# The gate and the squares of a grouped norm moved into the scan before it, its roots into the transposes

## The chip, the cores and the metric

The program runs on one core of a Trainium2 chip, as one launch. The metric is the device time of the execution in microseconds (us), the median of several runs. The engines are PE (TensorE, matmuls), DVE (VectorE), ACT (ScalarE), POOL (GpSimd) and SP (SyncE, which issues most transfers here). They run on their own and wait for each other by semaphores.

## What is computed

One layer of a diffusion backbone on 640 tokens (128 context and 512 latent tokens, five chunks of 128), all in float32. What matters here is the Mamba-2 branch, cut to the part around the change:

```python
y_f, h_f = _ssd_chunked(xh, dt[0], a_neg[0], bm, cm, h0_f)
y_r, h_b = _ssd_chunked(_flip_seq(xh), ...)
y = y_f + _flip_seq(y_r) + xh * d_skip
y = _group_rmsnorm(y * jax.nn.silu(z), norm_w, SSD_GROUPS)   # 4 groups of 512 of the 2048 channels
...
merged = sigmoid(gate_a) * (y_a @ w_branch_a) + sigmoid(gate_b) * (y_b @ w_branch_b)
```

`_group_rmsnorm` divides each group of 512 channels of a token by the root of its mean square (plus 1e-6) and multiplies by the weight of the channel. silu(z) was computed earlier and lies in DRAM (`silu_z`). After this branch come the output projection, a second norm, the router and the mixture of experts.

## The kernel before

The kernel is written by hand, stage by stage. A stage is one block in which each engine has its own list of instructions in program order; between two stages all engines meet. An engine works strictly down its list, so a wait holds up all that stands behind it. The three stages that matter follow each other:

- `stage_ssd`, the scan. It runs over 40 sub-steps, in the order of the list `subs`: chunk (0, then 4, 3, 2, 1), group of 512 channels, half of a group. Two sub-steps, a pair here, make one group of one chunk. In a sub-step j SP loads a row of decay sums, spread over the partitions, four sub-steps ahead (`spread`, L963, when `y_done` of j-4 frees the slot); ACT makes decays of it (eight L1185 and one L1188); DVE multiplies these into the matrix (L1273), and takes results from PSUM (L1256 or L1259, L1246); PE multiplies (L1144). POOL multiplies the skip term (L1031), scales rows for the sub-step two ahead (L1008), weighs rows for the states (L939, at even sub-steps until chunk 1), and adds up the finished output (`finish_y`, L1016 and L1019) into the tile `X`. Beside it PE computes rows of the modulation in 24 pieces (`at_sub` says behind which sub-steps), with weights that SP loads two pieces ahead (L955).
- `stage_norm_y`, here called the norm stage. Per chunk of 128 tokens it loads silu(z) (L1312), multiplies it into `X` (L1383 on DVE for chunk 0, L1323 on POOL for the others), squares and sums each group (L1344 on ACT), takes mean, reciprocal and root (L1372, L1374, L1349), scales the group by its root (L1380 on DVE), transposes its four blocks of 128x128 into one of eight PSUM banks (L1334), and takes them out as two parts, a rounded one and the rest, both multiplied by the norm weight (L1361 on ACT, L1393 on DVE). At its end come the two parts of the first block of branch weights, a unit (`split_hi`, L183 on ACT; `split_lo`, L191 on DVE; the whole unit is 128x2048 words).
- `stage_branch_b` multiplies the 2048 channels by `w_branch_b`, eight units, one after the other (L212 to L214, three matmuls for each product of two split operands), with each unit split while the one before is multiplied.

What sets the order is thus the text of the lists and the semaphores. PSUM has eight banks; `X` and the weights lie in SBUF.

## Time and profile before

| | us |
|---|---|
| median of 3 runs | 1619.68 (1617.15 to 1621.8) |
| time of the profiled execution | 1623.28 |
| its span, first to last instruction | 1621.5 |
| PE busy | 1359.6 (84%) |
| DVE busy | 830.5 (51%) |
| ACT busy | 669.1 (41%) |
| POOL busy | 265.7 (16%) |

The mean granted clock of PE is 0.898 of full speed (2.4 GHz); the clock has two levels, 1.0 and 0.5. Busy shares are means over stages that differ: in the stretch of the profile that is looked at below, from 712 us to 1119 us after the first instruction, the scan, the norm stage and branch B have other limits each. "Idle before" in a row is how long the engine stood still ahead of the instruction, and the name behind the arrow is what ended it.

### The profile page before, as it was taken

The page shows a single profiled execution, that of the slowest core. Times are in us where ns is not written, and L with a number is a line of the kernel's source. Part 1 is how long each engine was busy: PE and PEld are TensorE (multiplying, and loading weights), DVE is VectorE, ACT ScalarE, POOL GpSimd, SP SyncE. Part 2 cuts the span into 40 slices and gives each one's busy share as a digit, 9 for nine tenths or more (in the row PEclk, how much of TensorE's full clock was granted, in tenths as well). Part 3 has the DMA queues.
Part 4 walks back from the last instruction along what each step waited for, and adds up shares of the span by engine and source line. Part 5 has one row for each costly group of instructions (what it writes and reads, how often), then busy time and mean ns, then how long its engine had stood idle before and what let it go on. Part 6 is the DMA issues. An engine that isn't in the chain of part 4 may idle for free. (4 is left out here: it accounts for less than half of the span.)

```text
span 1621.5 us, 20620 instructions
## 1 busy us (share of the span) xinstructions
PE 1359.6 (84%) x7925; PEld 1190.4 (73%) x7925; DVE 830.5 (51%) x953; ACT 669.1 (41%) x1028; POOL 265.7 (16%) x284
## 2 busy tenths in 40 slices
PE   3999989799998999668888826999974499999980
PEld 1789989799997889645656625998772388888860
DVE  2411432277663111026677666332536189999966
ACT  2423321144442222155567536111131277777753
POOL 0600000000000010044579750000005000000002
PEclk9899999999999999877899856999967699999995
DMA  9982121122112332343454341224246499999945
GB/s 387 405 321 78 53 78 53 36 78 79 60 71 94 128 122 80 115 158 114 132 164 163 130 182 69 79 100 156 93 162 238 158 371 397 415 414 412 404 176 207
DMA packets 61639, 289.09 MB, mean 178 GB/s; under 512 B 8171, under 2 KB 12787, under 8 KB 41206
## 3 DMA queue, kind: packets, MB, share of 16 engines
q1 hardware_dynamic: 48566, 242.18, 40.0%
q0 software_dynamic: 12608, 45.62, 7.2%
q8 instruction: 56, 0.92, 0.2%
q14 instruction: 25, 0.20, 0.0%
q10 hardware_dynamic: 384, 0.16, 0.0%
HBM read 239.51 MB, written 48.43 MB: 178 GB/s over the span
## 5 line engine op out<-in xcount | busy, mean ns | idle before, releaser
L212 PE MATMUL banks<-rounded,rounded 128*128 128x320 f32 (+1 forms) x1168 | 366.8, 314 | 20.1 <-DVE rounded L735 6.9
L213 PE MATMUL banks<-rounded,rounded 128*128 128x320 f32 (+1 forms) x1168 | 364.6, 312 | 0.0
L214 PE MATMUL banks<-rounded,rounded 128*128 128x320 f32 (+1 forms) x1168 | 364.5, 312 | 0.0
L212 PEld LDWEIGHTS banks<-rounded,rounded 128*128 128x128 f32 (+1 forms) x1168 | 221.7, 190 | 21.6 <-issue 13.9
L191 DVE TENSOR_TENSOR rounded<-words,rounded 128x2048 fp32r<-128x2048 f32 x52 | 119.2, 2292 | 226.3 <-ACT rounded L183 224.1
L1889 DVE TENSOR_TENSOR rounded<-words,rounded 128x2048 fp32r<-128x2048 f32 x93 | 212.9, 2290 | 32.9 <-ACT rounded L1880 32.1
L213 PEld LDWEIGHTS banks<-rounded,rounded 128*128 128x128 f32 (+1 forms) x1168 | 221.8, 190 | 0.4
L214 PEld LDWEIGHTS banks<-rounded,rounded 128*128 128x128 f32 (+1 forms) x1168 | 221.5, 190 | 0.3
L1880 ACT ACTIVATE rounded<-words 128x2048 fp32r<-128x2048 f32 x96 | 183.6, 1916 | 46.6 <-PE banks L2007 39.2
L183 ACT ACTIVATE rounded<-words 128x2048 fp32r<-128x2048 f32 x52 | 99.2, 1908 | 140.7 <-PE banks L233 62.7
L1185 ACT ACTIVATE words<-words,words 128x128 f32<-128x128 f32 x320 | 97.8, 388 | 75.4 <-DMA words<-decay_sums 75.4
L1144 PEld LDWEIGHTS banks<-words 128*128 128x128 f32 x640 | 89.6, 221 | 44.8 <-issue 43.6
L231 PE MATMUL banks<-rounded,rounded 128*128 128x512 f32 x280 | 112.4, 402 | 10.7 <-PEq L632 6.7
L1144 PE MATMUL banks<-words 128*128 128x64 f32 x640 | 91.8, 305 | 34.5 <-DVE words L1273 34.5
L232 PE MATMUL banks<-rounded,rounded 128*128 128x512 f32 x280 | 111.5, 398 | 0.0
L233 PE MATMUL banks<-rounded,rounded 128*128 128x512 f32 x280 | 111.4, 398 | 0.0
L2005 PE MATMUL banks<-rounded,rounded 128*128 128x512 f32 x256 | 102.7, 401 | 2.7 <-issue 2.4
L2007 PE MATMUL banks<-rounded,rounded 128*128 128x512 f32 x256 | 100.9, 394 | 0.0
L2006 PE MATMUL banks<-rounded,rounded 128*128 128x512 f32 x256 | 100.9, 394 | 0.0
L854 POOL DMA_DIRECT2D silu_z<-words x20 | 10.9, 543 | 531.4 <-ACT words L834 531.4
L779 DVE SCALAR_TENSOR_TENSOR words<-words 128x642 f32<-128x642 f32 x96 | 85.3, 888 | 3.4
L231 PEld LDWEIGHTS banks<-rounded,rounded 128*128 128x128 f32 x280 | 54.3, 194 | 22.5 <-issue 11.2
(270 smaller groups left out, 2034.7 us busy)
## 6 DMA issues: line engine op xcount, KB each, us to landing
words<-in_units SPq DMA_DIRECT2D x52, 1024.0 KB, 4.9
words<-in_wg SPq DMA_DIRECT2D x32, 1024.0 KB, 8.1
words<-in_wu SPq DMA_DIRECT2D x32, 1024.0 KB, 8.6
words<-in_wd SPq DMA_DIRECT2D x32, 1024.0 KB, 9.4
words<-decay_sums SPq DMA_DIRECT2D x40, 512.0 KB, 3.7
words<-in_w_mod_rest SPq DMA_DIRECT2D x32, 512.0 KB, 5.0
slot_rows<-words POOLq DMA_DIRECT2D x27, 512.0 KB, 21.6
expert_rows<-words POOLq DMA_DIRECT2D x25, 512.0 KB, 9.6
```

Of the source, the lines that this page charges most:

```text
L191: self.nc.vector.tensor_tensor(self.lo[:, i % 2, :], self.raw[:, i % 2, :], self.hi[:, i % 2, :].bitcast(F32), ALU.subtract).then_inc(self ...
L212: nc.tensor.matmul(out, lhs[0](k), rhs[0](k), start=(k == 0), stop=False)
L213: nc.tensor.matmul(out, lhs[0](k), rhs[1](k), start=False, stop=False)
L214: last = nc.tensor.matmul(out, lhs[1](k), rhs[0](k), start=False, stop=(k == nk - 1))
L231: nc.tensor.matmul(out, rows[0], w[0][:, k, :], start=(kk == 0), stop=False)
L232: nc.tensor.matmul(out, rows[0], w[1][:, k, :], start=False, stop=False)
L233: last = nc.tensor.matmul(out, rows[1], w[0][:, k, :], start=False, stop=(kk == KD - 1))
L1144: last = nc.tensor.matmul(o, E[:, j % SLOTS, at:at + P], XT[:, 2 * (j % 3) + d, h * HD:(h + 1) * HD], start=(d == 0), stop=(d == 1))
L1880: self.nc.scalar.activation(self.hi[:, q % 3, :], self.raw[q], ACT.Copy).then_inc(self.hi_ready, 1)
L1889: (ops or self.nc.vector).tensor_tensor(self.lo[:, q % 3, :], self.raw[q], self.hi[:, q % 3, :].bitcast(F32), ALU.subtract).then_inc(self. ...
L2005: nc.tensor.matmul(o, HB[0][:, kk, :], hi[:, cols], start=(kk == 0), stop=False)
L2006: nc.tensor.matmul(o, HB[0][:, kk, :], lo[:, cols], start=False, stop=False)
```

## The change

1. In the scan, SP loads silu(z) group by group (`load_z`, 128x512, one tile `Z`, for 18 of the 20 groups, `GATED`), POOL multiplies it into `X` behind `finish_y` (`apply_z`), and ACT squares the product into the same tile `Z` and sums it (`squares`). The next load waits for these squares. At the scan's end DVE and ACT take mean, reciprocal and root for the first 16 groups (`ROOTED`).
2. In the norm stage the groups are no longer scaled. POOL multiplies the identity by a group's roots (`scales`, 128x128 each), and PE multiplies the blocks by that diagonal matrix: a plain matmul in place of the transpose. Only two groups are gated and squared here, and four rooted.
3. ACT and DVE take a bank of 512 columns out in one instruction each, in place of four, and without the norm weight.
4. The norm weight is multiplied into the eight units of branch weights by POOL (`w.scale`, 128x2048, in place), the first in the norm stage, the others in branch B, ahead of their split.
5. The loads of the first two units are issued at the start of the norm stage, not behind the loads of silu(z).

The core of the diff:

```diff
+GROUPS = [(c, g) for c in (0, 4, 3, 2, 1) for g in range(G)]
+GATED, ROOTED = 18, 16
...
+    def scale(self, pool, i, column):
+        i += self.first
+        pool.wait_ge(self.raw_loaded[i % 2], 16 * (i // 2 + 1))
+        v = self.raw[:, i % 2, :].rearrange("p (k n) -> p k n", k=KI)
+        self.nc.gpsimd.tensor_tensor(v, v, column.unsqueeze(2).broadcast_to([P, KI, UNIT // KI]),
+                                     ALU.mult).then_inc(self.scaled, 1)
...
@@ stage_ssd, SP @@
+            def load_z(i):
+                if i:
+                    sp.wait_ge(squared, i)
+                c, g = GROUPS[i]
+                sp.dma_start(Z, scr["z"][c * P:(c + 1) * P, cols(g)]).then_inc(z_loaded, 16)
...
             for j in range(NS):
                 if j + SLOTS < NS:
                     spread(j + SLOTS)
+                if j >= 3 and j % 2 and (j - 1) // 2 < GATED:
+                    load_z((j - 1) // 2)
                 if j in at_sub:
                     store_piece(at_sub[j] - 1)
@@ stage_ssd, POOL @@
+            def apply_z(i):
+                c, g = GROUPS[i]
+                if c:
+                    pool.wait_ge(y_whole, 2 * i + 2 - N0)
+                else:
+                    pool.wait_ge(y_steps, 2 * i + 2)
+                pool.wait_ge(z_loaded, 16 * (i + 1))
+                nc.gpsimd.tensor_tensor(X[:, c, cols(g)], X[:, c, cols(g)], Z, ALU.mult).then_inc(z_applied, 1)
...
                 if j > N0:
                     finish_y(j - 1)
+                if j and j % 2 == 0 and j // 2 <= GATED:
+                    apply_z(j // 2 - 1)
@@ stage_ssd, ACT @@
+            def squares(i):
+                c, g = GROUPS[i]
+                act.wait_ge(z_applied, i + 1)
+                nc.scalar.activation(Z, X[:, c, cols(g)], ACT.Square, accum_out=ssq[:, i:i + 1]).then_inc(squared, 1)
...
             for j, (c, g, q) in enumerate(subs):
+                if j >= 7 and j % 2:
+                    squares((j - 7) // 2)
                 act.wait_ge(sums_spread[j % SLOTS], 16 * (j // SLOTS + 1))
...
+            squares(GATED - 1)
+            act.wait_ge(mean_done, 2)
+            nc.scalar.activation(rr[:, 0:ROOTED], rr[:, 0:ROOTED], ACT.Sqrt).then_inc(root_done, 1)
@@ stage_norm_y, POOL @@
+            def scales(i):
+                nc.gpsimd.tensor_tensor(diag(i), ident, rr[:, i:i + 1].broadcast_to([P, P]), ALU.mult).then_inc(s_diag, 1)
+            for i in range(ROOTED):
+                scales(i)
+            for i in range(GATED, n):
+                c, g = GROUPS[i]
+                pool.wait_ge(s_z[i - GATED], 16)
+                nc.gpsimd.tensor_tensor(X[:, c, cols(g)], X[:, c, cols(g)], Z[:, i - GATED, :], ALU.mult).then_inc(s_y, 1)
+            pool.wait_ge(s_in, 16)
+            w.scale(pool, 0, nw)
+            pool.wait_ge(s_root, 1)
+            for i in range(ROOTED, n):
+                scales(i)
@@ stage_norm_y, PE @@
+            for i, (c, g) in enumerate(GROUPS):
+                pe.wait_ge(s_diag, i + 1)
+                if i >= 8:
+                    pe.wait_ge(s_lo, i - 7)
+                for q in range(4):
+                    k = 4 * g + q
+                    last = nc.tensor.matmul(ps[:, i % 8, q * P:(q + 1) * P], X[:, c, k * P:(k + 1) * P], diag(i), start=True, stop=True)
+                last.then_inc(s_tr, 1)
@@ stage_norm_y, ACT @@
+            for i, (c, g) in enumerate(GROUPS):
+                act.wait_ge(s_tr, i + 1)
+                nc.scalar.activation(hi[:, 4 * g:4 * g + 4, tokens(c)], turned(i), ACT.Copy).then_inc(s_hi, 1)
+                if i == 7:
+                    for k in range(GATED, n):
+                        m, h = GROUPS[k]
+                        act.wait_ge(s_y, k - GATED + 1)
+                        nc.scalar.activation(Z[:, k - GATED, :], X[:, m, cols(h)], ACT.Square, accum_out=ssq[:, k:k + 1]).then_inc(s_sq, 1)
+                if i == 9:
+                    act.wait_ge(s_ms, 2)
+                    nc.scalar.activation(rr[:, rest], rr[:, rest], ACT.Sqrt).then_inc(s_root, 1)
+            w.split_hi(act, 0, scaled=True)
@@ stage_branch_b @@
+        @block.gpsimd
+        def _(pool):
+            for i in range(1, 8):
+                w.scale(pool, i, nw)
...
-                if w.exists(i + 1):
-                    w.split_hi(act, i + 1)
+                w.split_hi(act, i + 1, scaled=i < 7)
```

How the lists of the engines change is shown at three places. In the scan, on POOL, one sub-step of an even number in chunk 2 reads as follows before (the names are SBUF regions by their first word; `words_50688_5414` is the region of the decays and the scaled rows, in the changed kernel of `Z` too):

```order
L1031 TENSOR_TENSOR words_33280_56<-words_20480_55,words_33280_56 128x256
L1008 TENSOR_TENSOR words_50688_5414<-words_20480_55,words_33280_56 128x512
L939 TENSOR_TENSOR words_52992_59<-words_20480_55,words_33280_56 128x512
L1016 TENSOR_TENSOR words_33280_56<-words_33280_56 128x256
L1019 TENSOR_TENSOR words_20480_55<-words_42496_49,words_33280_56 128x256
```

and in the changed kernel:

```order
L1067 TENSOR_TENSOR words_33280_56<-words_20480_55,words_33280_56 128x256
L1035 TENSOR_TENSOR words_50688_5414<-words_20480_55,words_33280_56 128x512
L957 TENSOR_TENSOR words_52992_59<-words_20480_55,words_33280_56 128x512
L1043 TENSOR_TENSOR words_33280_56<-words_33280_56 128x256
L1046 TENSOR_TENSOR words_20480_55<-words_42496_49,words_33280_56 128x256
L1056 TENSOR_TENSOR words_20480_55<-words_20480_55,words_50688_5414 128x512
```

One multiplication of 512 columns, L1056, has come behind the sums of every second sub-step, 18 times in all.

On SP, in a stretch of the scan in which the modulation's pieces stand at odd sub-steps, the list before is:

```order
L963 DMA words_50688_5414<-decay_sums 128x1024 x2
L955 DMA words_42496_49<-in_w_mod_rest 128x1024
L956 DMA words_42496_49<-in_b_mod 1x128
L985 DMA modulation<-words_42496_49 2x128
L963 DMA words_50688_5414<-decay_sums 128x1024 x2
```

and in the changed kernel:

```order
L981 DMA words_50688_5414<-decay_sums 128x1024 x2
L987 DMA words_50688_5414<-silu_z 128x512
L973 DMA words_42496_49<-in_w_mod_rest 128x1024
L974 DMA words_42496_49<-in_b_mod 1x128
L1010 DMA modulation<-words_42496_49 2x128
```

The load of silu(z), L987, and its wait for the squares of the group before have come between the decay sums and the modulation's weights. Where the pieces stand at even sub-steps, it stands alone between two loads of decay sums.

In the norm stage, on ACT, the list before begins (to the second chunk):

```order
L1344 ACTIVATE words_33280_56<-words_20480_55 128x512 x4
L1349 ACT_TABLE_LOAD
L1349 ACTIVATE words_33280_56<-words_33280_56 128x4
L1344 ACTIVATE words_33280_56<-words_20480_55 128x512 x4
L1361 ACTIVATE rounded_10240_8266<-banks,words_33280_56 128x128 x8
L1349 ACTIVATE words_33280_56<-words_33280_56 128x4
```

and in the changed kernel the whole of it is:

```order
L1406 ACTIVATE rounded_10240_8397<-banks 128x4x128 x8
L1411 ACTIVATE words_50688_5414,words_33280_56<-words_20480_55 128x512 x2
L1406 ACTIVATE rounded_10240_8397<-banks 128x4x128 x2
L1414 ACTIVATE words_33280_56<-words_33280_56 128x4
L1406 ACTIVATE rounded_10240_8397<-banks 128x4x128 x10
L199 ACTIVATE rounded_4096_50<-words_42496_49 128x2048
```

The squares ahead of the first transposed block are gone, and the 80 copies of 128 columns are 20 of 512.

## Rows read from the trace of the kernel before

**Rows 1.** Busy time by stretch: us, busy us of each engine (instructions), granted clock, DMA.

```profile
712.00:774.50 62.50, 50.36 (x269) 33.92 (x270) 35.61 (x61) 36.63 (x96) 26.42 (x27) 0.72 0.34 110
...
819.50:861.60 42.10, 35.70 (x276) 25.83 (x277) 29.34 (x51) 28.03 (x72) 34.23 (x38) 0.96 0.47 154
...
940.60:1000.60 60.00, 18.57 (x80) 15.96 (x81) 49.01 (x112) 38.82 (x128) 18.21 (x4) 0.53 0.32 123
```

**Rows 2.** Timeline of the norm stage: start us, duration us, engine, line; idle before.

```profile
940.69 1.05 SPq L1312 DMA_DIRECT2D words<-silu_z  x2
...
953.35 13.92 DVE L1380 TENSOR_SCALAR words<-words,words 128x512 f32<-128x512 f32 x4 [0.27 <-ACT words L1349]
...
990.60 3.68 PE L1334 MATMUL banks<-words,words 128*128 128x128 f32 x16 [3.42 <-DVE words L1380]
...
995.77 2.03 ACT L183 ACTIVATE rounded<-words 128x2048 fp32r<-128x2048 f32 x1
997.85 2.28 DVE L191 TENSOR_TENSOR rounded<-words,rounded 128x2048 fp32r<-128x2048 f32 x1
...
1000.60 0.60 PE L212 MATMUL banks<-rounded,rounded 128*128 128x320 f32 x1 [6.32 <-PEq L1306]
```

**Rows 3.** The same windows view, at lower and full clock of the PE.

```profile
692.30:696.00 3.70, 3.69 (x17) 3.70 (x18) 0.00 (x0) 0.60 (x1) 1.04 (x1) 0.50 1.00 388
698.90:701.00 2.10, 2.02 (x16) 1.86 (x16) 0.64 (x2) 0.60 (x1) 0.82 (x1) 1.00 0.59 164
...
1000.60:1006.60 6.00, 6.00 (x22) 6.00 (x23) 2.29 (x1) 1.74 (x1) 0.00 (x0) 0.50 0.84 300
```

**Rows 4.** Groups by line: busy us, mean ns | idle before; evictions of 512 columns.

```profile
L1213 DVE TENSOR_TENSOR words<-words,banks 128x512 f32<-128x512 f32 x24 | 16.5, 688 | 0.8
...
L1177 ACT ACTIVATE words<-banks 128x512 f32<-128x512 f32 x8 | 4.8, 598 | 12.7 <-DMA out_state<-words 7.1 <-PE banks L1056 5.6
```

**Rows 5.** Groups by line within the norm stage.

```profile
L1323 POOL TENSOR_TENSOR words<-words,words 128x2048 f32<-128x2048 f32 x4 | 18.2, 4575 | 10.9 <-DMA words<-silu_z 10.9
...
L1344 ACT ACTIVATE words<-words 128x512 f32<-128x512 f32 x20 | 12.9, 643 | 24.8 <-DVE words L1383 24.3
```

**Rows 6.** Windows of pairs of sub-steps at full clock, and the sum of the six tight ones.

```profile
819.50:829.60 10.10, 8.24 (x64) 5.97 (x64) 6.99 (x13) 7.00 (x18) 7.98 (x10) 1.00 0.46 151
...
861.60:870.30 8.70, 7.99 (x65) 6.27 (x65) 7.12 (x13) 6.42 (x18) 8.41 (x9) 1.00 0.55 172
...
sum 54.20, PE 47.17 PEld 36.94 DVE 40.36 ACT 38.70 POOL 52.48; mean PE 7.86 PEld 6.16 DVE 6.73 ACT 6.45 POOL 8.75
```

**Rows 7.** Timeline inside the tight pairs, the rows that the argument uses.

```profile
862.31 1.68 DVE L1273 TENSOR_TENSOR words<-words,words 128x1024 f32<-128x1024 f32 x1
...
862.87 1.60 POOL L1031 TENSOR_TENSOR words<-words,words 128x256 f32<-128x256 f32 x1
...
867.43 0.61 POOL L1031 TENSOR_TENSOR words<-words,words 128x256 f32<-128x256 f32 x1
...
868.00 1.04 POOL L1008 TENSOR_TENSOR words<-words,words 128x512 f32<-128x512 f32 x1
...
869.83 1.06 ACT L1188 ACTIVATE words<-words 128x1024 f32<-128x1024 f32 x1
...
872.92 0.73 POOL L1019 TENSOR_TENSOR words<-words,words 128x256 f32<-128x256 f32 x1
...
873.68 0.69 DVE L1246 TENSOR_TENSOR words<-banks,words 128x512 f32<-128x512 f32 x1 [0.98 <-POOL words L1019]
```

**Rows 8.** The page: DMA issues, KB each, us from issue to landing.

```profile
words<-decay_sums SPq DMA_DIRECT2D x40, 512.0 KB, 3.7
words<-in_w_mod_rest SPq DMA_DIRECT2D x32, 512.0 KB, 5.0
```

**Rows 9.** Transfers of the stored silu(z), whole chunks.

```profile
DMA to landing us min/median/max: 2.6/3.8/6.8
```

**Rows 10.** Timeline of branch B: VectorE's wait for the second unit's products.

```profile
1031.73 0.82 DVE L1443 TENSOR_TENSOR words<-banks,words 128x640 f32<-128x640 f32 x1 [7.42 <-PE banks L214]
```

More of the change, by code:

```diff
@@ L143, in __init__ @@
         self.used = kit.sem(f"{stream}_unit_used")
+        self.scaled = kit.sem(f"{stream}_unit_scaled")
     def section(self, n):
@@ L162, in __init__ @@
         self.raw_loaded, self.hi_ready, self.lo_ready = stream.raw_loaded, stream.hi_ready, stream.lo_ready
-        self.used = stream.used
+        self.used, self.scaled = stream.used, stream.scaled
     def to_load(self):
@@ L909, in stage_ssd @@
     y_whole = kit.sem("y_whole")
+    z_loaded, z_applied, squared, mean_done, root_done = (kit.sem("s_" + x) for x in ("z_loaded", "z_applied", "squared", "mean", "root"))
     rows_weighed = [kit.sem(f"s_weighed{j}") for j in range(2)]
@@ L1294, in stage_norm_y @@
     X = kit.at(O_X, NC, INNER)
-    Z = [kit.at(O_HL + o, INNER) for o in (UNIT, 3 * UNIT)]
+    Z = kit.at(O_HL + 6144, 2, GW)
     hi, lo = kit.rnd(O_H, KI, T), kit.rnd(O_BC, KI, T)
-    nw, ssq, rr = kit.at(O_TMP + 2560, KI), kit.at(O_TMP + 2580, NC * G), kit.at(O_TMP + 2600, NC * G)
-    sq = kit.at(O_TMP + 2656, GW)
+    nw = kit.at(O_NW, KI)
+    ssq, rr = kit.at(O_SQ, NC * G), kit.at(O_SQ + NC * G, NC * G)
+    early, late = kit.at(O_TMP + 2560, 12, P), kit.at(O_NW + KI, 8, P)
+    diag = lambda i: early[:, i, :] if i < 12 else late[:, i - 12, :]
     ident = kit.const("ident")
-    (s_in, s_y, s_ms, s_root, s_r, s_sq, s_tr, s_hi, s_lo) = (
-        kit.sem("n_" + x) for x in ("in", "y", "mean", "root", "scaled", "squares", "turned", "hi", "lo"))
-    s_z = [kit.sem(f"n_z{j}") for j in range(2)]
+    (s_in, s_y, s_ms, s_root, s_diag, s_sq, s_tr, s_hi, s_lo) = (
+        kit.sem("n_" + x) for x in ("in", "y", "mean", "root", "diagonal", "squares", "turned", "hi", "lo"))
+    s_z = [kit.sem(f"n_z{j}") for j in range(NC * G - GATED)]
     w = stream.section(0)
-    bank = lambda c, g: 4 * (c % 2) + g
+    n = NC * G
+    rest = slice(ROOTED, n)
+    cols = lambda g: slice(g * GW, (g + 1) * GW)
+    tokens = lambda c: slice(c * P, (c + 1) * P)
+    turned = lambda i: ps[:, i % 8, :].rearrange("p (q t) -> p q t", q=4)
     with nc.Block() as block:
@@ L1337, in _ @@
         @block.scalar
         def _(act):
-            def squares(c):
-                act.wait_ge(s_y, c + 1)
-                for g in range(G):
-                    if c or g:
-                        act.wait_ge(s_sq, G * c + g)
-                    nc.scalar.activation(sq, X[:, c, g * GW:(g + 1) * GW], ACT.Square,
-                                         accum_out=ssq[:, c * G + g:c * G + g + 1]).then_inc(s_sq, 1)
-            def root(c):
-                act.wait_ge(s_ms, 2 * c + 2)
-                nc.scalar.activation(rr[:, c * G:(c + 1) * G], rr[:, c * G:(c + 1) * G], ACT.Sqrt).then_inc(s_root, 1)
@@ L1351, in _ @@
-            squares(0)
-            root(0)
-            act.wait_ge(s_in, 16)
-            for c in range(NC):
-                if c + 1 < NC:
-                    squares(c + 1)
-                for g in range(G):
-                    act.wait_ge(s_tr, G * c + g + 1)
-                    for q in range(4):
-                        k = 4 * g + q
-                        nc.scalar.activation(hi[:, k, c * P:(c + 1) * P], ps[:, bank(c, g), q * P:(q + 1) * P],
-                                             ACT.Copy, scale=nw[:, k:k + 1]).then_inc(s_hi, 1)
-                    if g == 1 and c + 1 < NC:
-                        root(c + 1)
```

76 lines of the change are left out of this document (27 added, 49 removed).

## The prediction

> **What bounds the kernel now.** I read the busy time by stretch first, then the norm stage in the order of time, then the scan pair by pair, and last the rows that give prices. In [rows 1] the norm stage (940.6 to 1000.6 us) stands out: PE is busy for 18.57 of 60 us and its mean granted clock is 0.53. PE does no work there that takes long; it waits for scaled groups. From its first transfer at 940.69 to the first matmul of branch B at 1000.60 the stage takes 59.9 us [rows 2]. Its engines work one behind the other: load, gate, squares, root, scaling, transpose, two evictions. The scaling is worse than its work: four L1380 take 13.92 us while POOL gates the next chunk in the same time. The last transposes end at 994.28 (990.60 + 3.68); then come the split of the first unit, 995.77 to 997.80 on ACT and 997.85 to 1000.13 on DVE, and the barrier [rows 2].
>
> The scan is different. PE is busy for 35.7 of 42.1 us there, and POOL for 34.2 [rows 1]. In six pairs at full clock (861.6 to 899.5 and 909.5 to 925.8, 54.2 us in all) POOL is busy for 52.48 us, or 97% [rows 6]. It is the engine that sets those pairs: DVE's L1246 waits 0.98 us for POOL's L1019 [rows 7]. Part of its busy time is waiting too. L1031 takes 0.61 us alone and 1.60 us where DVE's L1273, which reads two SBUF operands, began before it, and L1273 itself takes 1.68 [rows 7]: such instructions of the two engines exclude each other. Other pairs (819.5 to 829.6 is one) take 10.1 us with POOL busy for 7.98 [rows 6], so they have 2.1 us of room; up to 774.5 there is more, POOL being busy for 26.4 of 62.5 us [rows 1].
>
> **The change, part by part: the norm stage.** The first diagonals need only roots from the scan. POOL's instruction with a broadcast operand takes 0.61 us for 256 columns and 1.04 for 512 [rows 7], so 128 columns should take 0.40. PE then starts about 1 us into the stage.
>
> PE has 20 x 4 multiplications by a diagonal. A plain float32 matmul is two instructions in the trace. The nearest rows are the states' matmuls, same shape: 17 instructions in 3.69 us at clock 0.5 (1.2 GHz), or 0.217 each, and 16 in 2.02 us at clock 1.0 (2.4 GHz), whose weight loads take 1.86, so 0.116 each [rows 3]. 160 instructions take 34.7 us at the lower level and 18.6 at the higher. After PE had stood still, the clock came back 3.7 us after matmuls without gaps began in one place and 6.0 in another [rows 3]. I take 5 us: 23 instructions at 0.217, 137 at 0.116 (15.9 us), together 20.9, so PE ends at 21.9 us.
>
> The other engines must keep below 0.93 us for each group. An eviction of 512 columns takes 0.60 us on ACT and 0.69 on DVE [rows 4]. POOL's 16 diagonals take 6.4 us. Two gatings follow: a multiplication of two full operands takes 4.575 us for 2048 columns [rows 5] and 0.73 for 256 [rows 7], by the line between them 1.28 for 512, so 2.6. The first unit of weights then takes 1.04 + 1536 x (1.04 - 0.61)/256 = 3.6 us (at most the 4.6 of [rows 5]), and four diagonals 1.6. They are there at 14 to 16 us, before PE reaches group 16 at about 18. The two squares hold ACT for 1.7 us, which eight banks cover. If they didn't, it would cost those 1.7.
>
> Behind PE stand the last eviction 0.6, the unit's split 2.0 and 2.3 [rows 2], and 0.47 to the first matmul (1000.60 - 1000.13): 5.4 us. Branch B starts 27.3 us into the stage in place of 59.9: **32.6 us less**. Bounds: 35 if the clock rises at once, 18.8 if it stays at 1.2 GHz (1 + 34.7 + 5.4 = 41.1).
>
> The Trainium skill speaks against the matmul: "TensorE: Matmul & The Clock Gate", Terms, says that the transpose mode is 4x faster for FP32. In the trace 16 transposes take 3.68 us at the lower clock [rows 2], 0.23 each, and a matmul 2 x 0.217 = 0.43: twice, not four times. By the page's rule the 80 would take 4 x 0.23 each, 73.6 us.
>
> **The scan.** POOL gets 18 multiplications of 1.28 us. The first four and some more fall into cold pairs with room: nothing. In the six tight pairs each lengthens the pair by its full time: 6 x 1.28 = 7.7 us. In the eight pairs from 774.5 to 861.6 the room of 2.1 us takes it in, but it shifts POOL's next instructions onto DVE's L1273, which stands between ACT's decays and PE's matmuls. What that costs lies between nothing and one instruction of about 1.0; I take 0.5 each: 4 us.
>
> The single tile `Z` makes a loop: load, gate, squares, next load. The squares stand in ACT's list behind the exponential for the sub-step three ahead, which ends at 870.89 (869.83 + 1.06); with 0.64 and about 0.2 for the sum they end at 871.7. The load takes 2.6 to 3.8 us for a whole chunk, four times a group [rows 9], so it lands at 874.3 to 875.5. POOL is ready for it at 873.65 (872.92 + 0.73) [rows 7]. So POOL waits 0.7 to 1.9 us at first, and less once the pair has grown by 1.28. SP waits for the squares too, and the modulation's weights stand behind it at the odd sub-steps. They go out some us later there, land 5.0 us after issue [rows 8], and PE wants them one pair (8.7 us) on, so of 3.7 us of slack most is used up; I take 2 us for both waits together. ACT has room for its squares (busy for 6.42 of 8.70 us [rows 6]). The mean and root at the end stand behind ACT's last exponential and beside PE's last products: nothing; the wait of DVE in front of its last two results is for squares long done. The scan's sum is 7.7 + 4 + 2 = **14 us more**, between 3 (half of the tight pairs' price) and 25 (1.8 us in each of fourteen pairs).
>
> **Branch B.** POOL weighs units 1 to 7, 3.6 us each. The first is ready 3.6 + 1.9 + 2.3 = 7.8 us into the branch, and unit 0 keeps PE busy for longer (DVE takes the products of the second unit 31.1 us after the branch began [rows 2, 10], so over 15 us for each); after that DVE has 7.42 us of idle time in each unit [rows 10], more than one such instruction can hold it up by exclusion. Nothing; without that cover up to 3.6 per unit.
>
> **The sum.** -32.6 + 14 = -18.6 us: the profiled execution of 1623.28 us (span 1621.5) would become 1604.7. Against the median of 1619.68, from which it differs by 3.6, I predict 1601.
>
> **Rivals.**
> - *The clock stays at 1.2 GHz in the norm stage.* For it: it was at 0.53 there; an uneven supply of diagonals or banks would leave gaps. Against it: PE works without gaps in this version, and in both rows of [rows 3] it rose. -18.8 + 14 = -5: 1615. The skill's page named above says under "PE-mode transpose" that transposes don't engage the full clock; the 0.53 of before fits that, and matmuls would escape it.
> - *The scan hides nearly all of it*, 0 to 4 us, because pairs that grow free POOL from its waits for DVE: -30: 1590. Against it stand the 97%.
> - *The loop through `Z` sets the scan.* If load, gate, squares and the place in ACT's list together exceed the pair in all 14 pairs from 774.5 on, POOL and then PE run at its pace. At 2.5 us each that is 35, and the kernel ends at 1622, on the other side. It decides from 2.3 us a pair (32.6 / 14). Against it: the lateness computed above is at most 1.9 us and shrinks as pairs grow.
> - *A float32 matmul costs four transposes.* The norm stage would take 1 + 73.6 + 5.4 = 80 us, 20 more than now, and with the scan the time is 1654. The two-for-one of the rows speaks against it. This is what the 4x of "TensorE: Matmul & The Clock Gate" would make here.
>
> **How the numbers follow.** Chances: my forecast 0.70, low clock 0.09, hidden scan 0.14, `Z` loop 0.05, four transposes 0.02. The forecast's own range is 1592 to 1610 (norm 30 to 35, scan 7 to 20). The range of 1589 to 1613 takes in the hidden scan's centre and leaves out most of the low clock. About 0.3%, or 4.9 us, is what a measurement of this kernel can tell from no change. Faster by more: the forecast and the hidden scan (0.84) and two thirds of the low clock (0.06), 0.90. Within it: the rest of the low clock and a little of the `Z` loop, 0.04. Slower: 0.06.
>
> **What the profile will show.** Norm stage: from SP's first transfer to the first matmul of branch B 27 us (25 to 30); plain matmuls in two levels, the clock rising 4 to 6 us in; last diagonals ahead of PE. Scan: 14 us longer, the growth in pairs that took under 9 us before; L1056 on POOL with 1.28 us and up to 2.3 where DVE excludes it; a wait of POOL for the load of silu(z) of under 1 us in the mean. Branch B as long as before. Wrong it would be by a stage that PE leaves at the lower clock, or by waits of PE for the modulation's weights or for L1321 of over 1.5 us a pair.

## The result, and the profile after the change

The changed kernel takes 1599.81 us in the median of four runs (1596.53 to 1606.38) against 1619.67 for the kernel before in the same job: the ratio is 0.9883, 95% interval [0.9844, 0.9922]. The prediction was 1601, range 1589 to 1613. A few executions that took far longer than the others of the same kernel (1832 us and more) are left out of all medians and ratios here. The profiled execution took 1596.53 us (span 1594.8), 26.7 us of span less than the profiled one of before. That difference has four parts, each a difference of start times in the two traces: the norm stage -33.3 us, what comes before it +8.5 (scan +7.5, its start +1.0), branch B -1.1, all that follows -0.8. How the -19.9 us between the medians divide is not known, since only one execution of each kernel was traced.

Busy time by stretch of the changed kernel; the columns are those of [rows 1]. The first line is the norm stage, the second the scan.

```profile
949.10:975.60 26.50, 20.88 (x160) 20.69 (x160) 16.26 (x23) 14.72 (x26) 13.34 (x24) 0.82 0.28 100
713.30:949.10 235.80, 192.50 (x1298) 139.60 (x1298) 145.39 (x244) 147.15 (x384) 185.81 (x179) 0.85 0.46 147
```

In [rows 1] PE was busy for 18.57 of 60 us of the norm stage. Now it is busy for 20.88 of 26.5. The timeline of that stage, to set beside [rows 2]:

```profile
949.17 0.83 SPq L1369 DMA_DIRECT2D words<-silu_z  x2
949.20 5.77 POOL L1377 TENSOR_TENSOR words<-words,words 128x128 f32<-128x128 f32 x16 [1.91 <-POOLq L84]
949.65 20.88 PE L1399 MATMUL banks<-words,words 128*128 128x128 f32 x160 [3.56 <-POOL words L1377]
...
962.80 1.48 POOL L1377 TENSOR_TENSOR words<-words,words 128x128 f32<-128x128 f32 x4 [1.27 <-ACT words L1414]
...
971.06 1.90 ACT L199 ACTIVATE rounded<-words 128x2048 fp32r<-128x2048 f32 x1
...
972.99 2.29 DVE L207 TENSOR_TENSOR rounded<-words,rounded 128x2048 fp32r<-128x2048 f32 x1 [1.11 <-ACT rounded L199]
...
975.75 0.61 PE L228 MATMUL banks<-rounded,rounded 128*128 128x320 f32 x1 [5.22 <-PEq L1364]
```

PE's 160 instructions are one row with nothing in it but work: 949.65 + 20.88 = 970.53. The last four diagonals are ready at 964.28 and PE needs the first of them after group 16. From 970.53 on, what is left is the last eviction, the unit's split and the barrier, 5.22 us. The clock by the windows view, to set beside [rows 3]:

```profile
949.70:955.30 5.60, 5.60 (x26) 5.60 (x27) 1.38 (x2) 1.32 (x3) 5.60 (x16) 0.50 0.82 263
957.00:965.00 8.00, 8.00 (x74) 8.00 (x73) 6.32 (x12) 6.36 (x14) 5.52 (x6) 1.00 0.13 54
```

An instruction takes 0.215 us at clock 0.5 and 0.108 at 1.0; the clock rose some 5.8 us after PE began. Groups of the norm stage by line, to set beside [rows 4, 5]:

```profile
L1422 DVE TENSOR_TENSOR rounded<-banks,rounded 128x512 fp32r<-128x512 f32 x20 | 13.6, 691 | 10.9 <-ACT rounded L1406 10.8
L1406 ACT ACTIVATE rounded<-banks 128x512 fp32r<-128x512 f32 x20 | 11.8, 596 | 12.8 <-PE banks L1399 12.8
L1377 POOL TENSOR_TENSOR words<-words,words 128x128 f32<-128x128 f32 x20 | 7.2, 406 | 3.2 <-POOLq L84 1.9 <-ACT words L1414 1.3
L188 POOL TENSOR_TENSOR words<-words,words 128x2048 f32<-128x2048 f32 x2 | 7.2, 3611 | 11.8 <-POOLq L1364 11.3 <-DMA words<-in_units 0.5
L1384 POOL TENSOR_TENSOR words<-words,words 128x512 f32<-128x512 f32 x2 | 2.5, 1287 | 0.0
```

In the scan, the waits from 772 us on, when the first of its pairs without much room begin, to its end (engine, line, what it waited for: us, times, longest). First the kernel before, then the changed one:

```profile
PE banks L1144 <- DVE words L1273: 20.3, 21, 1.7
...
DVE words L1246 <- POOL words L1019: 3.0, 2, 2.0
...
PE banks L1059 <- POOL words L939: 0.9, 1, 0.9
```

```profile
PE banks L1182 <- DVE words L1321: 20.9, 21, 2.2
...
POOL words L1056 <- DMA words<-silu_z: 13.6, 7, 4.5
DVE words L1294 <- POOL words L1046: 12.9, 10, 2.7
...
PE banks L1097 <- POOL words L957: 5.2, 4, 2.1
...
PE banks L1118 <- DMA words<-in_b_mod: 2.0, 2, 1.0
```

L1182, L1321, L1294 and L1097 are L1144, L1273, L1246 and L1059 of before. VectorE and PE wait for GpSimd in more places, PE waits for the modulation's bias and weights, which it never did before, and GpSimd stands 13.6 us for silu(z). One pair shows how this turns into time. It took 8.76 us before and takes 14.28 now:

```profile
875.27 2.01 DVE L1321 TENSOR_TENSOR words<-words,words 128x1024 f32<-128x1024 f32 x1
875.38 0.32 SPq L987 DMA_DIRECT2D words<-silu_z  x1
...
876.16 2.02 POOL L957 TENSOR_TENSOR words<-words,words 128x512 f32<-128x512 f32 x1
...
878.24 2.07 PE L1097 MATMUL banks<-words,words 128*128 128x512 f32 x2 [2.09 <-POOL words L957]
...
879.77 0.69 DVE L1294 TENSOR_TENSOR words<-banks,words 128x512 f32<-128x512 f32 x1 [2.16 <-POOL words L1046]
879.82 1.27 POOL L1056 TENSOR_TENSOR words<-words,words 128x512 f32<-128x512 f32 x1
...
882.24 2.62 PE L1182 MATMUL banks<-words 128*128 128x64 f32 x16
```

```profile
874.80:889.10 14.30, 10.86 (x67) 8.17 (x65) 8.88 (x13) 8.86 (x25) 13.79 (x15) 0.76 0.47 142
...
876.90:883.80 6.90, 5.56 (x16) 4.15 (x17) 3.52 (x7) 3.44 (x10) 6.67 (x7) 0.51 0.52 176
```

GpSimd comes to L957 late and needs 2.02 us for it beside VectorE's L1321, in place of the 1.05 it takes alone; PE stands for 2.09 us, up to 878.24. The mean clock over the pair is 0.76: it is at the lower level from 876.9 to 883.8 us, where the pair before the change had 1.00. POOL is busy for 13.79 of 14.3 us. No single wait makes the 5.5 us: two of some 2 us (PE's for L957, VectorE's for L1046) and the lower clock beside and behind them do. How much each of the three adds is not shown.

### The profile page after: what moved, and what is told of

It reads as the page before. It is cut to its first block and busy times, and to the rows that moved or that the text cites. A ratio compares the mean times of both kernels' runs of the same rounds, so it can differ in the third digit from the quotient of the medians.

```text
span 1594.8 us, 20703 instructions
## 1 busy us (share of the span) xinstructions
PE 1360.2 (85%) x8005; PEld 1191.6 (75%) x8005; DVE 802.3 (50%) x866; ACT 657.7 (41%) x965; POOL 320.2 (20%) x328
## 5 line engine op out<-in xcount | busy, mean ns | idle before, releaser
L228 PE MATMUL banks<-rounded,rounded 128*128 128x320 f32 (+1 forms) x1168 | 365.7, 313 | 18.7 <-DVE rounded L751 6.6
L1182 PEld LDWEIGHTS banks<-words 128*128 128x128 f32 x640 | 86.5, 215 | 45.9 <-issue 45.0
L1182 PE MATMUL banks<-words 128*128 128x64 f32 x640 | 88.9, 299 | 35.2 <-DVE words L1321 35.1
```

What stands on the lines that cost most here:

```text
L228: nc.tensor.matmul(out, lhs[0](k), rhs[0](k), start=(k == 0), stop=False)
L1182: last = nc.tensor.matmul(o, E[:, j % SLOTS, at:at + P], XT[:, 2 * (j % 3) + d, h * HD:(h + 1) * HD], start=(d == 0), stop=(d == 1))
```

## The experiments

The scan is counted here from the first matmul of y to the first transfer of the norm stage, the norm stage from there to the first transfer of branch B, each in the one profiled execution of its run. Pairs are numbered from 0 to 19; pair 13 is the one just shown. Ratios are to the kernel before in the same job.

| run | ratio, 95% interval | scan | norm stage |
|---|---|---|---|
| before | | 228.4 | 59.7 |
| changed | 0.9883 [0.9844, 0.9922] | 235.9 | 26.4 |
| e1_again | 0.9894 [0.9871, 0.9917] | 236.3 | 26.4 |
| e2_no_gate | | 226.7 | 26.0 |
| e3_free_z | 0.9867 [0.9846, 0.9888] | 239.9 | 26.1 |
| e4_transposes | | 243.9 | 22.4 |
| e5_no_multiply | | 232.2 | 25.2 |
| e6_gate_16 | 0.9877 [0.9859, 0.9896] | 236.4 | 26.5 |
| e7_gate_14 | 0.9864 [0.9843, 0.9885] | 241.4 | 26.7 |
| e8_norm_gates | 0.9925 [0.9905, 0.9945] | 224.7 | 47.4 |
| e9_scalar_loads | 0.9827 [0.9809, 0.9845] | 237.5 | 25.4 |
| e10_gate_12 | 0.9850 [0.9828, 0.9872] | 233.4 | 30.1 |
| e11_gate_12_scalar_loads | 0.9832 [0.9812, 0.9852] | 238.5 | 27.4 |
| e12_no_multiply_scalar_loads | | 225.1 | 24.9 |

The totals of e2 and e4 are not compared: the values decide how many blocks the experts' stage runs, and from its first instruction to its last it took 384 and 383 us there against 311 to 313 in before, the changed kernel, e5 and e12.

**e1_again**, the changed kernel once more.

> The changed kernel as it is, once more, beside the others of this call. My theory of the result (norm stage 33 us shorter, scan some 8 to 14 longer) expects 1597 to 1606 as its first four executions had. The rival that the scan's price is an accident of one execution expects a spread that reaches below 1594.

Its median is 1603.53 us, profiled 1594.05; the runs lie between 1594 and 1609. Two runs of the same kernel differ by 15 us where those of before keep within 7. The scan scatters most: 235.9, 236.3, and 243.9 in e4, whose scan has the same code. The kernel's first stage, the same in all runs, ended anywhere between 229.2 and 234.1 us in the fourteen profiled executions. And with before's code it took 228.4, and 224.7 in e8; 3.0 of the 3.7 us between those two are one pair, at clock 0.75 (13.55 us) in one and at 1.0 (10.55 us) in the other. So a difference of a few us between two profiled scans shows nothing by itself.

**e2_no_gate**, the scan without loads, gating and squares:

```diff
-            load_z(0)
...
-                if j >= 3 and j % 2 and (j - 1) // 2 < GATED:
-                    load_z((j - 1) // 2)
...
-                if j and j % 2 == 0 and j // 2 <= GATED:
-                    apply_z(j // 2 - 1)
...
-                if j >= 7 and j % 2:
-                    squares((j - 7) // 2)
...
-            squares(GATED - 1)
...
+            nc.vector.memset(ssq, 1.0).then_inc(squared, ROOTED)
```

> The changed kernel with the gating left out of the scan (no loads of silu(z), no multiplications on POOL, no squares for 18 groups; the sums of squares are set to 1). Theory: it is faster than the changed kernel by the scan's price, 8 to 14 us, so some 1587, and the scan takes as long as before (stage begins at 940.7 us again). Rival 'the scan hides it nearly all': at most 3 us faster. In the norm stage nothing changes: 26 to 27 us to the first matmul of branch B.

The scan took 226.7 us. Everything that the change puts into it costs the difference to 235.9, 236.3 and 243.9: 9 to 17 us, in the mean 12. The other two scans without it, 228.4 and 224.7, put that mean at 10 to 14. By the expectation 8 to 14 was to come; the rival, at most 3, is excluded.

**e3_free_z**, the squares to a tile of their own, so that a load waits for the gating alone:

```diff
-                    sp.wait_ge(squared, i)
+                    sp.wait_ge(z_applied, i)
...
-                nc.scalar.activation(Z, X[:, c, cols(g)], ACT.Square, accum_out=ssq[:, i:i + 1]).then_inc(squared, 1)
+                if i:
+                    act.wait_ge(squared, i)
+                nc.scalar.activation(squared_rows, X[:, c, cols(g)], ACT.Square,
+                                     accum_out=ssq[:, i:i + 1]).then_inc(squared, 1)
```

> The squares write to a tile of their own (bfloat16, read by nobody), so the load of silu(z) waits only for the multiplication before it. The loop through Z is broken, the work on POOL stays. If POOL's work and its exclusion with VectorE make the scan's price, it gains 0 to 2 us on the changed kernel. If the wait for the loads does (18.7 us in nine waits in the trace), it gains 5 us or more, and these waits are under 4 us in all.

The ratio is 0.9867 against 0.9883 and 0.9894, inside each other's intervals, and the scan took 239.9 us. GpSimd's waits for silu_z fell from 13.6 us to 6.8 and PE's for in_b_mod from 2.0 to at most 0.2, both from 772 us on. The intervals can't tell no gain from one of some 5 us, so neither of the two theories of the expectation is excluded by the time; the waits were to fall under 4 us and did not. What is excluded is the prediction's rival, a loop of load, gate and squares that sets the pace at 2.3 us a pair: the squares are out of it here, and nothing of the order of 30 us came back. A load still waits for the multiplication before it.

**e4_transposes**, the norm stage's matmul by a diagonal as a transpose:

```diff
-                    last = nc.tensor.matmul(ps[:, i % 8, q * P:(q + 1) * P], X[:, c, k * P:(k + 1) * P], diag(i), start=True, stop=True)
+                    last = nc.tensor.transpose(ps[:, i % 8, q * P:(q + 1) * P], X[:, c, k * P:(k + 1) * P], ident)
```

> The 80 multiplications by the diagonal are transposes by the identity again (so the output is not scaled by the roots); all else as in the changed kernel. By the rows of before a transpose takes half of a matmul: PE needs 17 us at the lower clock, against 20.9, and the kernel gains about 4 us. If transposes let the clock rise, the evictions on VectorE (0.69 us a group) set the stage and it gains 5 to 7. By the skill's factor of four the gain would be over 15 us at equal clock, which the evictions allow only down to 14 us in all.

Groups by line, and three windows of the stage:

```profile
L1399 PE MATMUL banks<-words,words 128*128 128x128 f32 x80 | 13.2, 344 | 7.1 <-POOL words L1377 7.1
...
L1425 DVE TENSOR_SCALAR words<-words 128x4 f32<-128x4 f32 x1 | 3.5, 3478 | 0.8 <-ACT words L1411 0.8
```

```profile
955.00:959.00 4.00, 4.00 (x21) 4.00 (x20) 2.15 (x4) 2.39 (x4) 4.00 (x12) 0.50 0.75 213
961.00:965.00 4.00, 3.12 (x29) 2.88 (x27) 3.15 (x4) 2.67 (x7) 3.37 (x3) 1.00 0.60 252
967.00:971.00 4.00, 3.38 (x16) 3.27 (x16) 4.00 (x8) 4.00 (x10) 1.47 (x4) 0.50 0.00 0
```

80 instructions in place of 160, of the same 0.11 us at full clock (3.12 / 29): twice, as the prediction had it, and not four times. The whole stage is only 4 us shorter, as PE then stood for 3.5 us, waiting for the last diagonals: the mean over four numbers on VectorE (L1425), which took 0.17 us in the changed kernel, took 3.48 beside GpSimd's 3.6 us of L188. The clock went to 1.0 in the middle of the transposes, so matmuls are not needed to raise it. It had been there for a moment in the kernel before too, whose norm stage has transposes alone:

```profile
979.30:982.70 3.40, 0.46 (x4) 0.22 (x2) 2.46 (x11) 3.40 (x15) 0.00 (x0) 1.00 0.01 2
```

**e5_no_multiply** and **e12_no_multiply_scalar_loads** leave the multiplications out of the scan; e12 issues the loads from ScalarE as well (the diff of e9).

```diff
-                if j and j % 2 == 0 and j // 2 <= GATED:
-                    apply_z(j // 2 - 1)
...
-                act.wait_ge(z_applied, i + 1)
+                if c:
+                    act.wait_ge(y_whole, 2 * i + 2 - N0)
+                else:
+                    act.wait_ge(y_steps, 2 * i + 2)
+                act.wait_ge(z_loaded, 16 * (i + 1))
```

> The 18 multiplications by silu(z) are left out of the scan; the loads, ACT's squares and the mean and root stay, and ACT's squares wait for the load and the finished group instead. So groups 0 to 17 are not gated, and as the values that later choose the experts differ, only the stretch up to the start of the output stage is compared. The scan (first y matmul to the norm's first transfer) was 235.9, 236.3 and 239.9 us with the gating and 226.7 without any of it (loads, squares and gating out), 228.4 before. Theory 1 (GpSimd's instructions are the price: their own 1.28 us and the exclusion with VectorE): without them the scan takes 227 to 230. Rival (the squares on ScalarE and the loads in front of the modulation weights carry it): 234 to 238. Norm stage 26.5 in both.

> The 18 multiplications of the scan are left out, and the loads of silu(z) are issued by ScalarE; the squares stay. Groups 0 to 17 are not gated, and only the stretch up to the output stage is compared. Theory 2 (SyncE's list was what made 232.2 us of 226.7): the scan takes 226 to 228.5 us and PE waits 0 us for in_b_mod. Rival (the squares in ScalarE's list, 0.64 us in front of the exponentials, or the transfers themselves): 231 to 233.

The scan took 232.2 us with the loads on SyncE and 225.1 with them on ScalarE, which is that of before or of e2. The first lies between the two theories of its expectation: something besides GpSimd's multiplications costs 5.5 us against e2, one execution of each. The timeline of e5 in pair 15, of 15.39 us (10.66 in e12), shows where some of it lies:

```profile
895.58 0.19 ACT L1222 ACTIVATION_READ_ACCUMULATOR words<-words 128x1 f32 x1
...
895.79 0.32 SPq L987 DMA_DIRECT2D words<-silu_z  x1
896.15 0.43 SPq L973 DMA_DIRECT2D words<-in_w_mod_rest  x1
896.63 0.29 SPq L974 DMA_DIRECT2D words<-in_b_mod  x1
...
900.81 0.64 PE L1116 MATMUL banks<-words,words 128*32 128x128 f32 x16 [1.59 <-DMA words<-in_b_mod]
```

The square ends at 895.77, silu_z goes out 0.02 us later, the weights behind it, and PE stands for them for 1.59 us. The mean clock of that pair was 0.61, and 1.00 in e12, so that of the 4.73 us between them the wait is only a part; that it brought the lower clock is not shown. In the whole run PE waited 4.7 us for in_b_mod, in e12 not at all; there the ACT queue issues silu_z and SyncE's weights pass it:

```profile
883.81 0.33 SPq L974 DMA_DIRECT2D words<-in_w_mod_rest  x1
...
885.71 0.33 ACTq L1217 DMA_DIRECT2D words<-silu_z  x1
```

e12 also frees `Z` from the squares, so that the two edits are not apart here. The squares and transfers themselves, which e12 keeps, cost nothing that shows. The totals of e5 and e12, which differ from each other in nothing but these two edits, were 1591.24 and 1582.55 us, one run each. The 7.1 us between the scans are thus one execution of each, where scans of one code have differed by 3.7 and by 8; the 4.7 us of waits for in_b_mod are the part that the trace shows.

**e6_gate_16** and **e7_gate_14** take two and four gatings out of the last pairs and do them in the norm stage.

```diff
-GATED, ROOTED = 18, 16
+GATED, ROOTED = 16, 16
...
-    Z = kit.at(O_HL + 6144, 2, GW)
+    Z = kit.at(O_HL + 6144, 4, GW)
```

> 16 groups are gated in the scan and four, not two, in the norm stage. The result is the reference's. Theory 1 (GpSimd's time in the last, tight pairs is the price, 1.28 us each with exclusions on top): pairs 17 and 18 lose one gating each, and behind the last pair the scan no longer ends with a square and a root behind ACT's last exponential: 1.5 to 3 us less. In the norm stage GpSimd has its first 16 diagonals at 6.4, four gated groups at 11.5, the scaled unit at 15.1 and the last diagonals at 16.7 us, still ahead of PE, which comes to group 16 at about 18: nothing. In sum 1.5 to 3 us faster than the changed kernel (1600): 1597. Rival (the scan's length is set by the clock's dips and not by one or two instructions): within 1 us of the changed kernel, with the same scatter.

> 14 groups are gated in the scan, six in the norm stage, and there the last diagonals go ahead of the scaling of the first unit. The result is the reference's. Theory 1: four of the tight pairs (15 to 18) lose a gating, 4 x 1.28 to 4 x 1.8 = 5 to 7 us less in the scan. In the norm stage the first 14 diagonals end at 5.6, six gated groups at 13.3, the squares at 14, the root at about 15.2, the last six diagonals at 15.6 to 17.6, when PE comes to group 14 at about 16 us, and the scaled unit at 21.2, when the split of it could begin at 21.5: 0 to 1.5 us more. In sum 4 to 6 us faster than the changed kernel: 1595. Rival (clock dips set the scan, or PE loses its clock where it waits for diagonal 14): no gain, or a norm stage of 29 to 31 us in place of 26.5.

The norm stage took them for nothing (26.5 and 26.7 us), as expected. The totals, 1599.35 and 1598.12, are not to be told from those of the changed kernel. In e7 pairs 16 to 18 took 7.80, 7.83 and 8.27 us (10.05, 7.53 and 9.57 before that edit), but pairs 7, 11 and 12 ran at clocks of 0.60, 0.57 and 0.69 and took 40.2 us in place of 30.6, in places where both kernels gate. The gain of 5 to 7 us did not come: pairs 16 to 18 gave 3.3, and those three took more. Of the 3.3, 2.25 are pair 16, whose clock was 1.00 in e7 and 0.66 in the changed kernel; it took the same 10.05 us at 0.66 in the kernel before, which has no gating there.

**e8_norm_gates**, the norm stage's part of the change alone: the scan is that of before, and gating and squares stay in the norm stage, by chunks. GpSimd's list there:

```diff
+            pool.wait_ge(s_y, 1)
+            for c in range(1, NC):
+                pool.wait_ge(s_z[c % 2], 16 * (c // 2 + 1))
+                nc.gpsimd.tensor_tensor(X[:, c, :], X[:, c, :], Z[c % 2], ALU.mult).then_inc(s_y, 1)
+                if c + 1 < NC:
+                    diagonals(c - 1)
+            pool.wait_ge(s_in, 16)
+            diagonals(NC - 2)
+            w.scale(pool, 0, nw)
+            diagonals(NC - 1)
```

> One part of the change alone: gating and squares stay in the norm stage, per chunk as before (the scan is that of before), and the norm stage has the diagonals, the merged evictions and the weight in the unit. The result is the reference's. The scan should take 227 to 228.5 us. In the norm stage GpSimd becomes the bound: its first gating begins at 3.8 us, four of 4.6 with diagonals of 1.6 between them end at about 27, then squares 2.6, mean and root 0.8, four diagonals 1.6, two us of matmuls and 5.4 to branch B: 39 to 41 us against 59.9 before and 26.5 after. So, if the gain of the change is mostly the taking away of the scaling and of the small evictions: 19 to 21 us faster than before (1600), the same as the changed kernel. Rival (without the gating in the scan the stage stays bound by the chain load, gate, squares, root): 50 us or more, 1610.

The scan was 224.7 us, the norm stage 47.4, not 39 to 41; the ratio is 0.9925, 1607.55 us. The timeline says why:

```profile
945.86 4.50 POOL L1374 TENSOR_TENSOR words<-words,words 128x2048 f32<-128x2048 f32 x1 [10.66 <-DMA words<-silu_z]
...
952.35 4.53 POOL L1374 TENSOR_TENSOR words<-words,words 128x2048 f32<-128x2048 f32 x1
953.75 3.15 DVE L1426 TENSOR_SCALAR words<-words 128x4 f32<-128x4 f32 x1 [3.15 <-ACT words L1402]
...
971.97 3.61 POOL L188 TENSOR_TENSOR words<-words,words 128x2048 f32<-128x2048 f32 x1
...
976.13 1.47 POOL L1369 TENSOR_TENSOR words<-words,words 128x128 f32<-128x128 f32 x4 [0.55 <-ACT words L1407]
```

The first gating on GpSimd began 7.8 us into the stage and not 3.8 (in the kernel before, with the same two loads of whole chunks, it began after 7.6), and the unit's 3.6 us stood ahead of the last diagonals. These two are the miss. So, of 33 us that the norm stage lost, 12 come from diagonals, merged evictions and the unit's weight and earlier load alone, and 21 more from having 18 groups gated before the stage; the latter costs 12 in the scan.

**e9_scalar_loads**, **e10_gate_12** and **e11_gate_12_scalar_loads** look for a better version. e9, in the scan:

```diff
-                if j >= 3 and j % 2 and (j - 1) // 2 < GATED:
-                    load_z((j - 1) // 2)
...
                 act.wait_ge(z_applied, i + 1)
+                if i + 1 < GATED:
+                    c1, g1 = GROUPS[i + 1]
+                    nc.scalar.dma_start(Z, scr["z"][c1 * P:(c1 + 1) * P, cols(g1)]).then_inc(z_loaded, 16)
+                if i:
+                    act.wait_ge(squared, i)
+                nc.scalar.activation(squared_rows, X[:, c, cols(g)], ACT.Square,
+                                     accum_out=ssq[:, i:i + 1]).then_inc(squared, 1)
```

e10 has `GATED, ROOTED = 12, 12`, and in the norm stage VectorE gates three groups after its first eviction and GpSimd five; e11 is both.

> The loads of silu(z) after the first are issued by ScalarE, right before it squares the group just gated, instead of by SyncE, and the squares go to a tile of their own, so that a load waits for the gating alone. SyncE's list is that of the kernel before. The result is the reference's. Theory 2 (a good part of the scan's price is in SyncE's list: its loads wait for squares, and modulation weights and sums stand behind them; without the multiplications but with those loads the scan took 232.2 us, without both 226.7): PE's wait for in_b_mod, 1.2 to 4.7 us in the runs with the loads on SyncE, goes to 0, silu_z lands earlier, and the scan takes 231 to 234 us against 235.9 to 239.9: 3 to 5 us less, 1596. Theory 1 (GpSimd's instructions alone are the price): scan 236 or more, 1600.

> 12 groups are gated in the scan, in the pairs up to 12; eight in the norm stage, three of them on VectorE and five on GpSimd. The result is the reference's. Theory 1: the seven last pairs (13 to 19) have no gating and take 66 to 68 us as before, against 69 to 74 in the profiled executions with 18 gatings; scan 230 to 233. In the norm stage GpSimd has its 12 diagonals at 4.8, its five gated groups at 11.2, the last diagonals from 12.9 to 16.1 and the unit at 19.7 us: 26.5 to 28 us. In sum 3 to 6 us faster than the changed kernel: 1595. Rival: what remains in the roomier pairs (SyncE's list, DVE's wait for L1046, clock dips after them) is the greater part of the price; the scan stays at 235 and the total at 1599, as it did with 16 and 14.

> Both edits together. The result is the reference's. If SyncE's list and the tight pairs are two separate prices, scan 227 to 230 us, norm stage 26.5 to 28, 1591 in all. If they are one and the same (whichever relieves the pairs), as the better of the two alone.

e9 is the fastest, 1592.58 us, ratio 0.9827 [0.9809, 0.9845]: 0.6% below the changed kernel, whose repeat has the interval [0.9871, 0.9917]. Against e3, which has the same tile for the squares and leaves the loads on SyncE, it is 0.4% below, with intervals that just fail to meet (0.9846 and 0.9845). Waits of its scan from 772 us on:

```profile
DVE words L1293 <- POOL words L1039: 16.4, 11, 4.0
...
POOL words L1049 <- DMA words<-silu_z: 2.9, 2, 1.5
```

silu_z is late for 2.9 us in place of 13.6 and the wait for in_b_mod is gone. But the one profiled scan took 237.5 us, no less than the changed kernel's; that execution was 4.5 us ahead of the changed kernel's before the second stage began, where both have the same code. So the medians show the gain, and the trace shows that its waits are gone, not that the scan is shorter. VectorE's waits for GpSimd's sums even grew, from 12.9 us to 16.4. Which wait the gain comes from is open: e3 had freed PE from all but 0.2 us of its wait for in_b_mod and was not clearly faster than the changed kernel.

e10's pairs 14 to 19, to the last matmul of y, took 49.4 us (56.7 in the changed kernel). They took 57.6 in the kernel before, which gates nothing there either, so the clock has a part in that. The norm stage took 30.1 us, not 26.5 to 28: the eight loads landed late, GpSimd waited 2.48 us for them, PE 1.93 us for the diagonals behind them, and PE's last 64 instructions took 9.04 us, 0.141 each and not 0.108, at a mean clock of 0.81. Total 1594.58. e11 is not the sum of both: 1596.28 us, by its ratio no better than e9 alone.

## Why the prediction was right

The mechanism of the norm stage came out as forecast, term by term. That of the scan came out in its size and its main cause, GpSimd's longer list (e9 against e12 below), and not in its places; that the median lies 1 us from the forecast is in part luck, since the changed kernel's own executions spread over 15 us.

- **Norm stage, -32.6 us**: measured -33.3 (59.9 to 26.6 by the prediction's marks, SP's first transfer to PE's first matmul of branch B; predicted 27.3). PE's 160 instructions took 20.88 us, predicted 20.9; the clock rose after 5.8 us, predicted 5, which the 133 instructions behind it, 0.114 us each and not 0.116, made good; the tail took 5.22, predicted 5.4. POOL's prices, all from lines through nearby rows, were 0.406 (0.40), 1.287 (1.28) and 3.61 (3.6). The squares cost nothing, with eight banks between PE and ACT.
- **Four transposes for one matmul**: excluded by e4: with the same shape it is two instructions against one. The Trainium skill ("TensorE: Matmul & The Clock Gate", Terms) calls the transpose mode 4x faster for FP32; e4 does not bear that out, and the measurement decides. The statement of the same page of the Trainium skill under "PE-mode transpose", that transposes don't engage the full clock, doesn't hold in e4 either, where the granted clock was 1.00 between 961 and 965 us; the 0.53 of before, which the prediction took to fit it, has a stretch at 1.00 in it too.
- **The scan, +14 us**: the size was about right, +7.5 in the profiled execution and 12 in the mean of three over e2. By places, in the profiled execution: the six tight pairs were to grow by 7.7 and grew by 8.1, and the eight ahead of them by 4 and grew by 4.0. That close agreement is luck: in e1 and e4, whose scans have the same code, the six grew by 9.3 and 11.6 and the eight by 6.2 and 6.8. The last pair gave 3.6 us back, which nobody forecast: its clock was 0.82 in place of 0.50 (to its last matmul of y it took 7.32 us in place of 10.84). Inside the six the price was not 1.28 each: they grew by 0.0, 5.5, 0.4, 1.3, 0.1 and 0.8. Where GpSimd's exclusion with VectorE (2.02 against 1.05) and two waits met, one pair paid for the others, partly at the lower clock. Nor did the eight pairs pay by the way that the prediction took, over PE's wait for L1321: from 772 us on that wait is 20.9 us in place of 20.3 (23.2 in e1, 21.7 in e4). What grew more is PE's wait for GpSimd's L957 (5.2 in place of 0.9) and VectorE's for L1046.
- **Both waits of `Z` together, 2 us**: this term was sized on a row misread. The 2.6 to 3.8 us of [rows 9] are the lowest and the median of a view that takes the 20 stores of silu(z) in with its loads; the five loads of whole chunks took 4.8 us, one of them 6.8, from issue to landing. That the loads of a group then took 3.0 to 4.9, but for the first, which is issued ahead of the scan, is near the forecast by luck. In the changed kernel GpSimd waited nine times for silu(z), 18.7 us in all and up to 4.5 at once, so slightly over 1 us for each of the 18 and not under 1; 12.2 of the 18.7 lie in front of the first six multiplications, where there is room. What the waits cost was hardly seen: in e3 they were 6.8 in place of 13.6 us from 772 us on, without a gain clear of the noise. The half of the term that the prediction named second, SyncE's list, may be the larger: PE's waits for in_b_mod were 2.0 us in the changed kernel and 4.7 in e5, the scans of e5 and e12 lie 7.1 us apart (one profile each), and moving the loads off the list gave 0.4% of the total between e3 and e9. The prices overlap with POOL's. Its multiplications by themselves cost 12.4 us where the loads are on ScalarE (e9 against e12, 237.5 and 225.1, which differ in nothing else) and 4 to 12 where they are on SyncE (the changed kernel's scans against e5, 232.2); the prediction's 7.7 + 4 was for this part.
- **Rivals**: the clock rose; the scan did not hide the gating; the loop through `Z` did not set it (e3; in the changed kernel's profile only one of the fourteen pairs grew by over 2.5 us); the matmul costs two.
- **Branch B as long as before**: 1.1 us shorter. Its first matmuls ran at the lower clock for 3.6 us, before the change for 6.0, and 2.4 us less at half the clock are worth 1.2.
- The profiled executions exaggerate: 26.7 us between them, 19.9 between the medians. The changed kernel's was its fastest of four, and that of before was slower than all the four others of its kernel.

What is open: where the clock falls. Identical code lost it in different pairs in each execution, and e7's gain went there; no run here holds it up through a scan. Of the two edits of e9, the tile was run by itself (e3), the queue was not. And the parts of the norm stage's change (diagonals, merged evictions, the weight in the unit, its earlier load) were run together only (e8).

## What to carry to other kernels

A DMA that waits on something is better kept out of an issuing list whose next transfers wait for nothing: the weights behind it kept PE waiting for 4.7 us in e5 and not at all in e12. What that is worth in time is less sure, 7.1 us of the scan in one profile each and 0.4% of the total between e3 and e9. Work moved into an earlier stage is free only where nobody waits for that engine's next instruction; elsewhere sum its time over the tight stretch and not by pair, and measure several times, since one execution can spend the price in one place. A multiplication by a scale per row before a transpose can ride on PE as a matmul by a diagonal at two transposes' price, and takes a whole pass of VectorE off the path.

## What the runs showed of the hardware that was not expected

- An instruction of VectorE on 128x4 elements took 3.15 and 2.09 us in e8 and 3.48 in e4, where it took 0.17 alone in the changed kernel. It stood beside a GpSimd instruction of 3.6 or 4.5 us and ended with it: in e8 956.90 against 952.35 + 4.53 = 956.88, in e4 966.64 against 966.62. So even such a small VectorE instruction on SBUF operands can be held until the end of GpSimd's. The exclusion was known from [rows 7] for large operands only.
- Identical scans took 235.9 to 243.9 us and differ in which pairs run below full clock (pairs 8 and 13 at 0.73 and 0.76 in the changed kernel, 8, 9 and 13 at 0.87, 0.74 and 0.86 in e1), and the totals of the changed kernel spread over 1594 to 1609 us.
- The clock reached 1.0 during transposes (e4, 961 to 965 us) as during matmuls.
